# First stage of a one-core kernel: blank products at the start, the first norm's root per token, and shifts put ahead of a copy

## The reference, cut to what matters

```python
h = rms_norm(x, norm_g[0]) * (1 + scale) + shift      # and the same for ctx
#   rms_norm(x, g) = x * rsqrt(mean(x * x) + EPS) * g
#   shift, scale, gate = split(silu(c) @ w_ada[0] + b_ada[0], 3)
px = h @ w_in[0]
km, vm = split(rms_norm(mem, g_mem) @ w_mem_kv)        # of it only vm here
```

## Time and profile before

| | |
|---|---|
| median of 3 runs | 1074.33 us (1072.66 to 1074.78) |
| time of the profiled execution | 1075.27 us |
| its span | 1073.4 us |
| TensorE busy | 1039.9 us, 97% |
| VectorE busy | 397.1 us, 37% |
| ScalarE busy | 333.3 us, 31% |
| mean granted clock of TensorE | 0.993 |

### The profile page before, as it was taken

One profiled execution on the slowest core, in us unless ns is written; L12 is line 12 of the kernel. 1 busy time (PEld: TensorE's weight loads), 2 busy tenths in 40 slices (PEclk: granted clock), 3 DMA queues, 4 the chain that ended last, 5 costly groups with the idle time before them and its releaser, 6 DMA issues.

```text
span 1073.4 us, 13331 instructions
## 1 busy us (share of the span) xinstructions
PE 1039.9 (97%) x4980; PEld 665.0 (62%) x4980; DVE 397.1 (37%) x1194; ACT 333.3 (31%) x782; POOL 14.1 (1%) x60
## 2 busy tenths in 40 slices
PE   6999999999999999999999999999999999999995
PEld 2444554544466777888888556788888844444441
DVE  5448535344243755363932004841112320000004
ACT  5132134334033246344454013750101311111112
POOL 0000000000000000000000000000000000000010
PEclk9999999999999999999999999999999999999998
DMA  9989424762233331453444442129646699999995
GB/s 364 422 305 362 180 78 164 289 254 81 76 118 117 116 120 41 176 199 118 136 148 151 154 157 79 40 104 426 255 157 235 237 394 422 422 423 423 424 422 221
DMA packets 33774, 241.84 MB, mean 225 GB/s; under 512 B 3792, under 2 KB 4048, under 8 KB 7760
## 3 DMA queue, kind: packets, MB, share of 16 engines
q1 hardware_dynamic: 30208, 212.87, 50.9%
q10 hardware_dynamic: 2928, 26.03, 6.5%
q0 software_dynamic: 576, 2.10, 0.5%
HBM read 234.70 MB, written 20.97 MB: 238 GB/s over the span
## 4 chain that ended last, share of the span: by engine, by line
PE 91%; DVE 3%; DMA 3%; ACT 2%; issue 1%; DVEq 0%; POOLq 0%; POOL 0%; SPq 0%; ACTq 0%
PE lin L501 24%; PE aux L501 10%; PE lin L970 9%; PE lin L601 7%; PE sc L525 6%; PE aux L970 5%; PE aux L861 4%; PE sc L637 4%; PE aux L665 3%; PE sc L935 3%; PE sc L501 3%; PE lin L651 3%; PE lin L680 2%; PE sc L575 1%; PE sc L734 1%; PE lin L734 1%
## 5 line engine op out<-in xcount | busy, mean ns | idle before, releaser
L501 PE MATMUL lin<-H,ring 128*128 128x256 f32 (+1 forms) x1104 | 267.8, 405 | 2.5 <-ACT PR L1305 2.5
L501 PEld LDWEIGHTS lin<-H,ring 128*128 128x128 f32 x1104 | 211.7, 192 | 57.3 <-issue 27.1
L501 PE MATMUL aux<-Y,ring 128*128 128x512 f32 (+1 forms) x256 | 83.4, 487 | 0.1
L601 PE MATMUL lin<-ring,H 128*128 128x384 f32 (+2 forms) x224 | 76.2, 502 | 0.0
L525 PE MATMUL sc<-H,ring 128*128 128x512 f32 (+1 forms) x192 | 70.4, 503 | 0.0
L501 PEld LDWEIGHTS aux<-Y,ring 128*128 128x128 f32 x256 | 48.4, 190 | 34.2 <-issue 28.8
L1682 DVE SCALAR_TENSOR_TENSOR UN<-UN,cols 128x512 f32<-128x512 f32 (+1 forms) x120 | 64.5, 610 | 0.0
L1183 ACT ACTIVATE SP<-lin 128x512 f32<-128x512 f32 (+2 forms) x88 | 42.0, 485 | 68.7 <-PE lin L651 68.7
L601 PEld LDWEIGHTS lin<-ring,H 128*128 128x128 f32 x224 | 40.8, 193 | 34.9 <-issue 22.4
L1606 DVE CUSTOM_DVE_ANT_0 SP<-sc,CW,SK 128x512 f32<-128x512 f32 (+1 forms) x48 | 31.8, 661 | 66.1 <-PE sc L637 66.0
L1194 ACT ACTIVATE SP<-SP,ST 128x513 f32<-128x513 f32 (+4 forms) x88 | 53.8, 611 | 6.7 <-DVE ST L1609 6.4
(11 more groups left out here) (329 smaller groups left out, 1202.2 us busy)
## 6 DMA issues: line engine op xcount, KB each, us to landing
ring<-w_stream SPq DMA_DIRECT2D x119, 1024.0 KB, 4.9
SP<-w_stream SPq DMA_DIRECT2D x13, 1024.0 KB, 21.0
UN<-w_stream SPq DMA_DIRECT2D x10, 1024.0 KB, 19.9
PR<-w_stream SPq DMA_DIRECT2D x8, 1024.0 KB, 22.3
CW<-w_stream SPq DMA_DIRECT2D x8, 1024.0 KB, 22.1
X<-w_stream SPq DMA_DIRECT2D x8, 1024.0 KB, 24.1
Y<-w_stream SPq DMA_DIRECT2D x8, 1024.0 KB, 18.7
PR<-ada_in SPq DMA_DIRECT2D x5, 1024.0 KB, 26.0
```

The source lines that it names most:

```text
L501: m = mm(dst, w[:, k, :], rhs(k), start=n == 0, stop=n == KT - 1)
L601: m = mm(bank[:, 0:width], src[:, k, tt * P:(tt + 1) * P], w[k // 4][:, k % 4, 0:width], start=k == 0, stop=k == KT - 1)
```

## The change

- GpSimd first clears `NB[:, 1536:1792]`; TensorE waits for it and makes 13 products of 128x256 from these zeros, into `sc[:, 0, 0:256]`, before its first real product. Nothing reads them.
- The product of step 4 becomes four products with one column each (mean squares per token on the partitions, 128x4). ScalarE takes the root of 128x4, VectorE its reciprocal and multiplies the identity by each of the four columns (4 times 128x128, into `RS`), and a 128x512 product of a tile of ones with `RS` spreads the result; ScalarE copies it into `RI`.
- The memory's values of tile 0 are cut otherwise around this: k = 4 ahead of the wait for the squares, 5 and 6 behind the four products, 7 behind the spreading product. For tile 1, only k = 4 stands ahead of `ada_folded(0)`.
- ScalarE makes the shifts of b = 0 before the copy L1238.
- The memory's norm on VectorE goes behind the shifts of b = 1, and the five transfers of ScalarE's queue behind those of b = 2 and `ada_block(3)`. What SyncE loads, and in which order, is unchanged.

```diff
+            pe.wait_ge(blank_ready, 1)
+            for _ in range(13):
+                mm(sc[:, 0, 0:256], NB[:, 1536:1664], NB[:, 1536:1792], start=True, stop=True)
...
-            memory_values(banks, w, 0, (4, 5))
+            memory_values(banks, w, 0, (4,))
             pe.wait_ge(sq_added, 2 * (KT - 1))
             at["sq"] = 2
-            mm(sc[:, 1, 0:512], t0("ones_d"), SA[:, :], start=True, stop=True).then_inc(first_ms, 1)
-            memory_values(banks, w, 0, (6, 7)).then_inc(lin_ready, 1)
+            for x in range(4):
+                m = mm(sc[:, 1, x:x + 1], SA[:, x * P:(x + 1) * P], t0("ones_d")[:, 0:1], start=True, stop=True)
+            m.then_inc(first_ms, 1)
+            memory_values(banks, w, 0, (5, 6))
+            pe.wait_ge(roots_spread, 1)
+            mm(sc[:, 1, 0:512], t0("tri")[:, P:2 * P], RS[:, :], start=True, stop=True).then_inc(spread_ready, 1)
+            memory_values(banks, w, 0, (7,)).then_inc(lin_ready, 1)
             pe.wait_ge(silu_c, 1)
             ada_block(0)
-            memory_values(banks, w, 1, (4, 5))
+            memory_values(banks, w, 1, (4,))
             ada_folded(0)
-            memory_values(banks, w, 1, (6, 7)).then_inc(lin_ready, 1)
+            memory_values(banks, w, 1, (5, 6, 7)).then_inc(lin_ready, 1)
...
-            pe.wait_ge(first_root, 2)
+            pe.wait_ge(first_inverse, 1)
...
-            fn(RS[:, :], sc[:, 1, 0:512], ACT.Sqrt, bias=col("eps")).then_inc(first_root, 1)
+            fn(ST[:, 0, :], sc[:, 1, 0:4], ACT.Sqrt, bias=col("eps")).then_inc(first_root, 1)
+            act.wait_ge(spread_ready, 1)
+            fn(RI[:, :], sc[:, 1, 0:512], ACT.Copy).then_inc(first_inverse, 1)
...
-            fn(MO[:, 1, :], take()[:, :], ACT.Copy, scale=RV[:, 1, 1:2]).then_inc(lin_taken, 1)
             for b in range(ADA_BLOCKS):
...
+                if b == 0:
+                    fn(MO[:, 1, :], take()[:, :], ACT.Copy, scale=RV[:, 1, 1:2]).then_inc(lin_taken, 1)
                 if b < ADA_BLOCKS - 1:
                     ada_block(b + 1)
-                if b == 1:
+                if b == 2:
                     act.wait_ge(lin_taken, TT)
                     act.dma_start(mv_kept, MO.rearrange("p t n -> p (t n)")).then_inc(mv_stored, 16)
...
+            nc.gpsimd.memset(NB[:, 1536:1792], 0.0).then_inc(blank_ready, 1)
             nc.gpsimd.memset(SC[:, :, :], 0.0).then_inc(sc_zeroed, 1)
...
-                    for s in range(2):
-                        n_inverse = step(v.reciprocal(RI[:, s * SEQ:(s + 1) * SEQ], RS[:, s * SEQ:(s + 1) * SEQ]))
+                    after(step(v.reciprocal(ST[:, 1, :], ST[:, 0, :])))
+                    dve.wait_ge(c0_in_s, 16)
+                    for x in range(4):
+                        ins = v.tensor_scalar(RS[:, x * P:(x + 1) * P], t0("ident"), ST[:, 1, x:x + 1], None, ALU.mult)
+                    ins.then_inc(roots_spread, 1)
+                    dve.wait_ge(first_inverse, 1)
                     for b in range(ADA_BLOCKS):
-                        after(n_inverse)
...
-                        if b == 0:
+                        if b == 1:
                             dve.wait_ge(mem_root, 1)
```

More of the change, by code:

```diff
@@ L305, in build @@
         ada_landed = [sem(f"ada_landed{b}") for b in range(ADA_BLOCKS)]
+        blank_ready, roots_spread, first_inverse, spread_ready = (
+            sem(n) for n in ("blank_ready", "roots_spread", "first_inverse", "spread_ready"))
         mem_first, mem_scaled, first_ms, first_root, m_inverse, mod_ready, open_ready, open_taken, mv_stored, mv_in = (
```

## The result

The change makes the kernel slower: 1078.06 us median (1076.8 to 1079.47, 7 runs) against 1074.33 (1072.66 to 1075.24, 7 runs), ratio 1.0041 with a 95% interval of 1.003 to 1.0051. Measured again beside the other kernels of the study it was 1.0030 (1.0016 to 1.0044). The prediction was no change, 1074.9, with a range from 1073.5 to 1077.3; it was wrong.

What follows compares the result with a forecast made beforehand. TensorE, busy 97% of the span, was taken to bound the kernel. Opened products starting at 32.41 instead of 31.81 add 0.6 us to the median 1074.33, giving 1074.9, range 1073.5 to 1077.3.

Steps and rivals of the forecast that it cites:

- The gate: TensorE's wait for VectorE's last squares, ending 20.56 us: earliest effective start 20.93 instead of 21.50, so 0.57 us visible gain.
- The opening: First memory values (L680), after the blanks: 6.88 + 0.23 us at full pace, ending at 15.9 to 16.8 instead of 18.90.
- The work behind the gate: TensorE's products after the wait for the squares: 10.62 us against 8.97 before, ending at 31.55 against 30.47.
- The root per token: After the four one-column products: spread root ready at 22.97 to 23.71, TensorE waiting from 23.44; cost taken as nothing.
- The copy that takes the place of the wait: Ahead of the opened products: TensorE waits 0.86 us for copy L1238 instead of 1.34, starting at 32.41 against 31.81.
- rival A: Clock falls in TensorE's new idle time, half pace behind the squares' wait: 1.7 us more, 1076.6; chance 0.24.
- The moved transfers: ScalarE's five issues take 5 x 0.5 us, to 60.7; shifts behind are due at 60.8, none held, 0.1 to spare.
- rival C: The moved transfers' constants land late, at 88.2, and TensorE's L756 waits 12.5 us more: 1087.4; chance 0.02.
- rival B: At the start, zeros do not lift the clock; TensorE reaches the squares' products 3.2 us late: 1078.1; chance 0.04.
- D: Slow pace at the start lasts longer in ordinary runs of the kernel before: no loss or small gain, 1073.9 to 1074.4; chance 0.12.

Runs made afterwards that it cites:

- the late bank: Kernel before with b = 0 shifts ahead of copy L1238 and TensorE's second lin bank taken only before its first writing product: median 1071.23 against 1072.85, ratio 0.9981.

## Why the prediction was wrong, point by point

- **The gate** was right: TensorE was ready early and went on at 20.77, for a last square at 20.73; the earlier opening bought idle time and nothing else. The opening itself was right too (blanks done at 8.4, within the wait for the first weights, and L682 at 0.43 from its first record). The blanks were forecast to end at 9.7 and the real products to start at 8.82 to 9.7; they started at 8.90.
- **The work behind the gate** was right: 10.62 forecast. Without the fall the version without blanks takes 10.6 from the effective start, and the start at 32.2 to 32.6 fits the 32.4.
- **The root per token** was right in its own terms: VectorE had the roots spread at 23.80, before TensorE came to its wait at 26.01, and without the fall, in the version without blanks, at 22.84 against 23.25. So no wait was added. Its price is the 0.79 behind the gate. Whether it makes the fall likelier is open.
- **The copy that takes the place of the wait** was right: 0.86 forecast, 0.80 measured (35.13, the end of TensorE's last value, to 35.93), and gone with the late bank.
- **The step that failed** is the forecast over rival A, "the clock falls in the new idle time". I gave it 0.24. The sum went on at full pace behind the new idle time, and the clock did not: it fell in both profiled executions of the changed kernel and, by the times, in half or more of the timed ones. The rival named the mechanism and the place, but its price was half of what it is: I took the 3.4 us of the stretch near 325 us, and the one here lasted 6.8, from 21.1 to 27.9, so it cost 3.4 and not 1.7. The argument against it, that each gap is shorter than the 2.5 us after which the earlier trace rows shows a fall, was no good. Gaps of 1.89 and 0.84 with one product between went ahead of the same fall, and in the other profiled execution a single one of 1.92. Nor is the earlier trace rows a rule in the other direction: in six of the twelve profiled executions the clock held after the same 2.5 us.
- **The moved transfers** were the second term that failed, by their size: I took 5 x 0.5 us of issue from the earlier trace rows, with 0.1 to spare, and they took 1.2 to 1.9 for the last ones. TensorE's wait for it, forecast at nothing, was 1.2 in the changed kernel and 0.5 in the one with this edit alone. The prediction's cushion, a product of TensorE still to be made (1.8 us), absorbed the rest. I had taken the length of an issue as a constant of the instruction, and it is not.
- **The constants** (rival C) and the **unlifted clock** (rival B) did not happen. 1078.1, the time of B, is the measured one by accident.
- **D** has nothing for it: in the four profiled kernels without blanks the opening takes 10.08 (before), 9.54, 9.69 and 10.19 us, so the slow pace at the start is nowhere a microsecond or two longer. The groups in the times of the kernel before, 1.7 to 1.9 us apart, fit the stretches at half pace near 325 and 500 us that some executions lack.

The measured sum, for the two profiled executions: 0.6 for work behind the gate, about 0.2 for squares that ended later (20.73 against 20.56), 3.4 for the fall, 1.5 for the hold, less the 1.7 of chance at 500 us: 4.0 against 3.8.

## What to carry to other kernels

Before TensorE's start is made faster, look at what it will wait for next: an early finish ahead of a fixed gate is idle time, and idle time can cost the clock, which is worse than the slow pace that it replaced. A long queue of waits (a bank taken before it is needed, a copy ahead of a shift) is the cheaper thing to mend: two small edits there brought the start forward by 1.3 us and the median down by 1.6. And when transfers are moved on an engine that also computes, price their issues as unknown, up to four times those of the old place, and keep them behind the work that others wait for.

## What the runs showed of the hardware that I had not expected

- TensorE's clock fell to 0.50 after idle stretches of 1.89 and 0.84 us with one product between, and in another execution after a single one of 1.92. It stayed there for 6.8 us of almost unbroken work. The same 2.5 us of idle time near 322 us was followed by a fall in six of twelve profiled executions. So by these rows an idle stretch of about 2 us can bring the fall and need not. The Trainium skill (TensorE: Matmul & The Clock Gate, Why this matters for your kernels) warns of idle gaps between bursts that are longer than these; here shorter ones went ahead of a fall.
- The granted clock fell without any wait of TensorE near 500 us in the kernel before (0.71 over five microseconds, all of them busy). It is there in ten of the twelve profiled executions. Each such stretch costs 1.7 us, which fits the groups of times of the kernel before, at about 1071, 1072.7 and 1074.5. That they are the reason for the groups is argued and not shown: a single execution of that kernel was profiled, 1075.27 with two stretches.
- The same five issues on ScalarE's queue took 0.34 to 0.50 us each at 47 us and up to 1.90 each at 51 us or later, in each of the kernels that issued them then. They are slow where they land soonest (8.8 us for the last one in the changed kernel, 12.9 in the earlier trace rows). One thing goes with it in the traces: at 47 to 50 us only SyncE's queue moved packets, and ScalarE's own began at 50; in the changed kernel from 62 us on nearly all packets were of ScalarE's own queue. I did not settle what slows them; it is not the order of the memory's norm, and at 51.8 us, in the version with the transfers back, SyncE's loads were still in flight when an issue took 1.19, so an empty machine is not the whole of it.
